# The turned branch outputs and the turned memory begin at a multiple of 128 bytes, the weight ring stays 96 bytes past one

## What is computed

```
for l in range(DEPTH):                      # first block; the second has the same outline
    x = x + 0.5 * swiglu(rmsnorm(x, ...), w_ffn1_in[l], w_ffn1_out[l])
    ...
    y_mla = mla_branch(...) @ w_o_mla[l]
    y_hg = hgrn2_branch(...) @ w_o_hg[l]
    mem_n = rmsnorm(mem, mem_norm[l])
    y_mem = memory_branch(mq, mem_n, w_mem_kv[l]) @ w_o_mem[l]
    merged = gates[:, :, 0] * y_mla + gates[:, :, 1] * y_hg + gates[:, :, 2] * y_mem
    x = x + merged @ w_out[l]
    x = x + 0.5 * swiglu(rmsnorm(x, ...), w_ffn2_in[l], w_ffn2_out[l])
```

## The kernel before

| region | begins before | past a multiple of 128 | of 256 |
|---|---|---|---|
| `OT`, `OT_upper`, `memory_rest` (`overlay`) | 204,768 | 96 | 224 |
| `ring` and `rest` (`slots`) | 180,192 | 96 | 224 |
| `Sc`, `hT_upper` (`steps`) | 163,808 | 96 | 224 |
| `upper` (from below, for comparison) | 4,320 | 96 | 224 |
| `xT_upper`, `xT_rest` (from below) | 45,312 and 53,504 | 0 | 0 |

## Time and profile before

### The profile page before, as it was taken

One profiled execution on the slowest core, in us unless ns is written; L12 is line 12 of the kernel. 1 busy time (PEld: TensorE's weight loads), 2 busy tenths in 40 slices (PEclk: granted clock), 3 DMA queues, 4 the chain that ended last, 5 costly groups with the idle time before them and its releaser, 6 DMA issues.

```text
span 2621.8 us, 48248 instructions
## 1 busy us (share of the span) xinstructions
PE 2583.0 (99%) x19726; PEld 2371.5 (90%) x19726; DVE 868.4 (33%) x1518; ACT 1285.9 (49%) x1934; POOL 2032.4 (78%) x906
## 2 busy tenths in 40 slices
PE   7999999999999999999999999999999999999998
PEld 6999999899899989989989998998998989899897
DVE  2644364211232436411121133733122131473212
ACT  4445555444444555544444444745444444574443
POOL 7988666798898856788888886468888878547886
PEclk9999999999999999999999999999999999999999
DMA  6566543555656654666655556245556556525664
GB/s 235 186 202 200 185 137 130 194 191 188 211 183 198 204 181 137 166 195 187 190 197 187 184 188 214 91 161 193 192 179 205 191 177 194 193 98 174 196 190 139
DMA packets 128738, 474.79 MB, mean 181 GB/s; under 512 B 14432, under 2 KB 14432, under 8 KB 127520
## 3 DMA queue, kind: packets, MB, share of 16 engines
q1 hardware_dynamic: 124704, 454.09, 53.1%
q0 software_dynamic: 3840, 17.83, 2.4%
HBM read 469.24 MB, written 2.62 MB: 180 GB/s over the span
## 4 chain that ended last, share of the span: by engine, by line
PE 91%; DVE 5%; ACT 2%; DMA 1%; issue 1%; POOL 1%; DVEq 0%; SPq 0%; ACTq 0%; POOLq 0%
PE psA L381 51%; PE psY L381 38%; PE psT L432 2%; DMA ring<-in_weights 1%; DVE psY L1279 0%; POOL rest L1065 0%; ACT upper L1876 0%; DVE psY L1267 0%; PE psT L654 0%; DMA cst<-in_consts 0%; DVE st L1364 0%; DVE x L1294 0%; ACT xT_upper L1876 0%; ACT G L1907 0%; DVE Sc L1339 0%
## 5 line engine op out<-in xcount | busy, mean ns | idle before, releaser
L1065 POOL TENSOR_TENSOR rest<-ring,upper 128x1024 fp32r<-128x1024 f32 (+1 forms) x834 | 1992.8, 2409 | 524.5 <-ACT upper L1876 513.9
L1876 ACT ACTIVATE upper<-ring 128x1024 fp32r<-128x1024 f32 (+1 forms) x834 | 870.2, 1053 | 787.4 <-DMA ring<-in_weights 786.9
L381 PE MATMUL psA<-xT_upper,upper 128*128 128x256 f32 x2784 | 383.1, 280 | 0.6 <-ACT arena L1876 0.6
L381 PE MATMUL psA<-xT_upper,rest 128*128 128x256 f32 x2784 | 381.1, 279 | 0.0
L381 PE MATMUL psA<-xT_rest,upper 128*128 128x256 f32 x2784 | 381.1, 279 | 0.0
L1320 DVE TENSOR_TENSOR psA<-sil,psA 128x256 f32<-128x256 f32 x144 | 61.8, 429 | 936.4 <-ACT sil L1876 936.3
L381 PEld LDWEIGHTS psA<-xT_upper,upper 128*128 128x128 f32 x2784 | 359.3, 188 | 12.8 <-ACT arena L1876 1.3
L381 PEld LDWEIGHTS psA<-xT_rest,upper 128*128 128x128 f32 x2784 | 349.4, 188 | 0.0
L381 PEld LDWEIGHTS psA<-xT_upper,rest 128*128 128x128 f32 x2784 | 349.4, 188 | 0.0
L381 PE MATMUL psY<-upper,hT_upper 128*128 128x512 f32 x704 | 202.6, 393 | 1.9 <-DVE hT_rest L1322 1.9
L381 PE MATMUL psY<-upper,hT_rest 128*128 128x512 f32 x704 | 200.4, 390 | 0.0
(11 more groups left out here) (282 smaller groups left out, 3003.7 us busy)
## 6 DMA issues: line engine op xcount, KB each, us to landing
ring<-in_weights SPq DMA_DIRECT2D x862, 512.0 KB, 3.8
G<-in_rows POOLq DMA_DIRECT2D x6, 1024.0 KB, 7.5
G<-in_rows POOLq DMA_DIRECT2D x7, 512.0 KB, 6.6
arena<-rel_by_distance POOLq DMA_DIRECT2D x8, 256.0 KB, 7.4
x<-in_x SPq DMA_DIRECT2D x2, 512.0 KB, 6.1
par<-in_params POOLq DMA_DIRECT2D x4, 256.0 KB, 5.6
xn<-in_mem POOLq DMA_DIRECT2D x1, 1024.0 KB, 11.1
memory_transposed<-arena POOLq DMA_DIRECT2D x1, 1024.0 KB, 5.5
```

Source lines behind the costliest of these rows:

```text
L381: i = pe.matmul(out, lhsT, rhs, start=start, stop=stop)
L1065: pool.tensor_tensor(rest[:, r, 0:n], ring[:, r, 0:n], upper[:, r, 0:n], ALU.subtract)\
L1876: act.activation(out, in_, func, **kw).then_inc(*up)
```

## The change

Two constants move. `SB_END` becomes 96 bytes smaller, and 32 bytes are left free between the ring and `OT`.

```
-SB_END = 229344
+SB_END = 229248
...
         overlay = SB_END - 4 * 6 * 4 * S
-        slots = overlay - 4 * R * PIECE
+        slots = overlay - 32 - 4 * R * PIECE
         steps = slots - 4 * 16 * S
```

## The result

The change made the kernel slower: 2632.69 us median (2631.05 to 2636.63, 7 runs) against 2621.86 us (2619.8 to 2624.64, 7 runs). The ratio is 1.0041, 95% interval 1.0029 to 1.0053. Forecast were 2617.3 us and a range up to 2621.5. The forecast started from 2620.41 us, the median of the first three runs of the kernel before; with seven runs it is 2621.86.

A forecast was written before the change was run, and what follows sets the result against it. TensorE's own stream was taken to bound the kernel. Branch products, keys and values summed to -3.8 us or, at the slower pace, -2.3; the middle, -3.1 from 2620.4, gave 2617.3 us, own range 2616.6 to 2618.1, wider range 2613.6 to 2621.5.

The forecast's parts named there:

- What bounds the kernel: TensorE's own stream, busy 99% of the span, sets the time; the change acts through its pace or by slowing another engine.
- Branch products: 1152 matmuls with OT moving each save 3.3 or 2.1 ns, 3.8 or 2.5 us in all.
- Keys and values: The memory's keys, 192 matmuls, save 0.6 or 0.4 us; the memory's values, 96 matmuls, lose 0.6 us.
- Cover: GpSimd still makes rest parts in time for faster branch products, which use at most 0.4 us of a 2.4 us lead.
- the tightest place: Early in merge, the first of six rest parts ends 2.4 us before TensorE starts the pass that needs it.
- I cost this at nothing: hT, Sc, PT, ring and rest move down 128 bytes, keep their 96 past a multiple of 128, and cost nothing.
- The slower rival: Place within 256 bytes counts: 3600 matmuls, xT moving over rest, go from 116.7 to 120.0 ns; 2629.3 us, chance 0.10.
- The argument against that rival: Pieces with two 416-column tiles, at 224 and 96 within 256: 190 ns each against 189 scaled, so place doesn't show.
- The multiple of 128: OT moving from a multiple of 128 instead of 96 past it runs at 116.7 or 117.9 ns, not 120.0.
- The rival without an effect: The moving operand's start costs nothing, OT is slower for another reason; 2620.4 us, at most 2621.0; chance 0.12.

The follow-up runs named there:

- e6: Kernel before with upper, x, xT, ring, rest, hT and OT all moved by 128 bytes modulo 256, all distances kept; 2620.72 us, ratio 0.9998.
- e2: Kernel before with ring, rest, hT, Sc and PT 128 bytes lower, OT where it was; 2632.41 us, ratio 1.0039.
- e9: The change plus before_upper 128 bytes larger, bringing upper to 96 and xT to 128 modulo 256; 2618.42 us against 2621.73, ratio 0.9985.
- e8: Kernel before with OT moved to 96 modulo 256, ring and hT kept at 224; 2621.84 us, ratio 1.0001.
- e1: Kernel before with OT moved as in the change, ring and hT 256 bytes lower and so still at 224; 2619.45 us against 2622.64, ratio 0.999.
- e5: Kernel before with OT moved to 0 modulo 256, ring and hT kept at 224; 2619.43 us against 2622.05, ratio 0.9988.
- e4: Kernel before with ring and rest moved to 96 modulo 256, hT moved by 256 bytes, OT where it was; 2631.23 us, ratio 1.0037.
- e3: Kernel before with only hT, Sc and PT moved, hT to 96 modulo 256; 2628.59 us, ratio 1.0024.
- e10: Kernel before with OT moved to 32 modulo 256, ring and hT kept at 224; 2617.67 us, one run.
- e11: Kernel before with OT moved to 64 modulo 256, ring and hT kept at 224; 2624.2 us, one run.
- e7: Kernel before with the weights and hT moved by 128 bytes modulo 256, xT left at 0 and OT at 224; 2637.6 us, ratio 1.0065.
- e12: Kernel before with OT moved to 192 modulo 256, ring and hT kept at 224; 2619.83 us, one run.

## Why the prediction was wrong

**What bounds the kernel: right.** TensorE's waits in total stayed, and the change acted through the pace of its stream alone.

**Branch products: right in size.** Forecast were 25.2 to 25.5 us per stretch and a saving of 2.5 to 3.8 us; measured 25.32 us, and 2.3 us for the class, the wait below included. The reason given for it was not right, and nor was that these become the same pair as `xT` over the weights: that holds modulo 128, but modulo 256 only for the pass over `rest` (distance 32). Over `upper` it is 160.

**Keys and values: right in kind.** -0.4 us (forecast -0.4 to -0.6) and +0.4 us (forecast +0.6); the keys' groups are at 0.95 us and not 0.93 to 0.94, the values' at 0.94 and not 0.93.

**Cover: held but for 0.33 us.** In the second layer's `merge` the timeline after the change has one wait for a rest part, which was not there before:

```profile
1099.07 0.73 PE L381 MATMUL psA<-OT_upper,rest 128*128 128x256 f32 x4 [0.33 <-POOL rest L1065]
```

I had called the first layer's fifth product the tightest place. The second layer's seventh was, in this execution. The faster branch products are not shown to be the reason: the chain goes from this wait back to the transfer of the piece, 12.32 us long, and e6, whose branch products still take 120.0 ns, waits 1.12 us at this place. No other engine's slowing reached TensorE.

**"I cost this at nothing": the step that failed.** `hT`, ring and `rest` keep their 96 past a multiple of 128, and I took that as all that counts. Their place within 256 changed from 224 to 96, while `upper` and `xT` stayed where they were. That broke the distances: `hT` under `upper` went from 0 to 128, `xT` over `rest` from 32 to 160. It cost 7.5 us in `hT`'s products and 2.9 us in `xT`'s. Not all of it is a pass's own new distance: `rest,hT_upper` kept distance 0 and yet went from 226.8 to 231.6 ns, 3.4 us in its 703 matmuls. e2 shows this half of the change alone to have the ratio 1.0039, and e9 takes the loss away by moving the two partners, with ring and `hT` left in place.

**The slower rival came nearest, at a chance of 0.10, and its price was about right by accident.** That the place within 256 bytes matters was right. It put all of the loss on `xT` moving over stationary `rest`, 3600 matmuls at +3.3 ns, +12.0 us. Measured, these 3600 lose about 1 ns each (117.9 ns from 116.8), and the larger part of the loss is in `hT`'s products, which it did not name. Its net, 2629.3 us, was still 3.4 us short, 1.5 us of them by the lower median it started from.

**The argument against that rival was a test that could not fail.** The pieces with two tiles of 416 columns have the moving weights at 224 and at 96 within 256, over stationary `xT` at 0: distances 224 and 96. Neither is the distance 0 of `hT`'s products, and with 512 columns the rows already had 232.5 ns for `xT` stationary and 227 for `hT`. Both tiles were at a slow distance, so their being equal said nothing on what leaving distance 0 costs. The rows held a sign of it: weights at 96 past 128 moved faster over `hT`, at the same place, than over `xT`. I read that as a property of the stationary operand alone.

**The multiple of 128.** I explained the saving by alignment of the moving operand. It is not enough: e8 changes the pace without a multiple of 128, and e1 and e5, both at a multiple of 128, have different paces (118.2 and 117.2 ns over all 1152 matmuls, waits left out).

**The rival without an effect.** It had a chance of 0.12, and the ratio of 1.0041 (1.0029 to 1.0053) excludes it. Its rule, the isolated distance between starts in the Trainium skill, TensorE: Matmul & The Clock Gate, section Back-to-back issue gap, has no term for an address; the paces here, 113.3 to 120.0 ns with 256 columns, differ by where the operands begin. The same page of the Trainium skill, section Step-by-step: what each phase is for, says that TensorE has two independent read ports in SBUF, one for the moving and one for the stationary operand. The traces don't show such independence in the pace: with the moving `OT` left in place, moving `rest` alone (e4) takes `OT_upper` over `rest` from 120.0 to 116.7 ns, and with the stationary operand left in place, moving `OT` changes the pace by up to 6.7 ns. Whether the ports have a part in it no run here shows.

**What stays open.** Why the distance matters; no run here looks into the memory. Whether it is the distance alone for steps under 128 bytes: in every kernel here the weights begin 96 past a multiple of 128, and the only common shift tried was 128 bytes (e6, and e9 against e5). So the paces at 32, 64, 96, 160 and 224 could as well hang on the moving operand's own place modulo 128, beside the distance. The loss in `hT`'s and `xT`'s products doesn't depend on that, since their distances changed by 128.

Open too is how one pass's pace depends on its neighbours: e3 has all three of `hT`'s passes off distance 0, yet its `hT` class costs less (492.1 us) than after the change (494.0), where only two are. And e3 and e4 apart multiply to 1.0061 where e2, both together, has 1.0039 (1.0026 to 1.0053). The `hT` class does add up in the traces (+5.6 and +2.2 us, and +7.6 in e2); the excess is in `xT`'s class (+0.7 and +3.7, and +0.7 in e2) and in the four runs of e4 that have no trace.

## What to carry to other kernels

When a stream of matmuls sets the time, look at addresses in pairs: before moving a buffer, write down for each product where the moving and the stationary operand begin modulo 256 bytes, and keep the difference. (Shown here for fp32r streams, and for moves by 128 bytes.) A buffer placed from the top drags all that is placed below it, so after such an edit list the new places of everything that moved, and of the partners that did not. And before a row is taken as evidence against a rival, ask whether it could have come out otherwise if the rival were right.

## What the runs showed of the hardware

The pace of 256 moving fp32r columns over a stationary 128 x 128, from the stretch of 216 matmuls in `merge` in those layers where the chain has it as one piece, `OT` at one distance from both `upper` and `rest`. The weights are 96 past a multiple of 128 throughout:

| distance | kernel | us for 216 | ns each |
|---|---|---|---|
| 0 | before, e6 | 25.92 | 120.0 |
| 32 | e5, e9 | 25.20 and 25.45 | 116.7 and 117.8 |
| 64 | e10 | 24.48 and 25.44 | 113.3 and 117.8 |
| 96 | e11 | 25.92 | 120.0 |
| 128 | e7, e8 | 25.63 and 25.64 | 118.7 |
| 160 | e1 | 25.35 to 25.83 | 117.4 to 119.6 |
| 224 | e12 | 25.56 | 118.3 |

Moves by 256 bytes changed nothing (ring and `hT` in e1: 226.8 ns for `rest,hT_upper`, as before). With 512 moving columns it is the other way round: distance 0 is the fast one where all three passes have it (226.8 to 230.4 ns by pass, before), and the other distances seen give 231 to 234 ns, but for the first pass of e3 (230.7). Next to passes at distance 128, one at distance 0 is as slow (231.6 ns after the change). Some distances have two paces in one program, which hold for a whole stretch: e10's stretch of 216 took 24.48 us in one layer and 25.44 us in two others, and e5 and e9 took 25.20 us in the two layers of the first block and 25.45 us in the two of the second. With all passes at distance 0 the first group of four in a down piece takes 0.927 us and the third 0.907 (medians, before).
